# RWKV chunk recurrence: the right-hand side of the solve as one 128-row product, alphas and state copied beside masked keys and values

## What is computed

```python
def step(S, inp):
    r_t, k_t, v_t, w_t, kk_t, a_t = inp
    sa = jnp.einsum('bhij,bhj->bhi', S, -kk_t)
    S = S * w_t[:, :, None, :] + sa[..., None] * (kk_t * a_t)[:, :, None, :] + v_t[..., None] * k_t[:, :, None, :]
    return S, jnp.einsum('bhij,bhj->bhi', S, r_t)
```

## Time and profile before

| | us |
|---|---|
| median of 3 runs | 1393.52 |
| lowest and highest of them | 1392.38 and 1394.54 |
| the profiled execution | 1392.71 |
| its span, first to last instruction | 1390.9 |
| stretch of the recurrence | about 540 to 716 |

### The profile page before, as it was taken

The page is one execution under the profiler, slowest core; times in us unless marked ns, Lnnn a source line. Parts: engine busy times, 40 slices in busy tenths (PEclk is TensorE's granted clock), DMA queues, the critical chain, the costliest instruction groups (busy, mean ns, idle before and its releaser), DMA issues.

```text
span 1390.9 us, 28090 instructions
## 1 busy us (share of the span) xinstructions
PE 1329.4 (96%) x12121; PEld 987.0 (71%) x12121; DVE 700.9 (50%) x1122; ACT 491.5 (35%) x797; POOL 176.8 (13%) x216
## 2 busy tenths in 40 slices
PE   5899999999999997999999999999999999998997
PEld 1789999999999997888888998844444444433443
DVE  3423235553326665655676667725455444454454
ACT  2423235545665555555544343211000100000113
POOL 2000000000112333333433001000000000000000
PEclk9999999999999999999989999999999999999999
DMA  9557522225532220000243565999999999999993
GB/s 331 194 197 235 174 78 76 77 76 147 150 110 77 76 61 26 4 4 4 67 128 97 172 214 181 333 408 408 409 428 425 426 427 428 424 427 426 426 428 152
DMA packets 132920, 310.62 MB, mean 223 GB/s; under 512 B 13314, under 2 KB 98536, under 8 KB 119864
## 3 DMA queue, kind: packets, MB, share of 16 engines
q1 hardware_dynamic: 122078, 285.86, 54.6%
q10 hardware_dynamic: 7546, 15.58, 3.1%
q0 software_dynamic: 3168, 7.33, 1.5%
HBM read 299.88 MB, written 12.79 MB: 225 GB/s over the span
## 4 chain that ended last, share of the span: by engine, by line
PE 49%; DMA 7%; DVE 2%; ACT 1%; issue 1%; SPq 0%; DVEq 0%; ACTq 0%; POOLq 0%
PE bank L3039 13%; PE bank L2858 7%; PE bank L3063 6%; DMA lower<-in_expert_w_up 4%; PE bank L3083 4%; PE bank L2886 3%; DMA upper7b<-in_expert_w_up 2%; PE bank L1778 2%; PE bank L498 2%; PE bank L3050 1%; PE bank L3013 1%; ACT upper L1575 1%; PE bank L1844 1%; PE bank L1825 1%; PE bank L1776 1%
## 5 line engine op out<-in xcount | busy, mean ns | idle before, releaser
L953 PE MATMUL bank<-upper2end 128*128 128x272 f32 x3168 | 413.7, 291 | 5.6 <-DVE upper2end L1183 5.4
L953 PEld LDWEIGHTS bank<-upper2end 128*128 128x128 f32 x3168 | 402.1, 189 | 20.1 <-issue 19.0
L3039 PE MATMUL bank<-upper7b 128*64 128x512 f32 x784 | 230.7, 596 | 7.3 <-issue 4.2
L1160 DVE TENSOR_TENSOR upper2end<-upper,upper2end 128x1024 fp32r<-128x1024 f32 x66 | 84.8, 1284 | 250.1 <-ACT upper2end L718 249.9
L3039 PEld LDWEIGHTS bank<-upper7b 128*64 128x64 f32 x784 | 69.8, 137 | 116.5 <-issue 116.2
L3039 PE MATMUL bank<-lower,upper7b 128*64 128x512 f32 x240 | 108.6, 596 | 2.3 <-issue 1.0
L2726 ACT ACTIVATE lower<-bank 128x256 f32<-128x256 f32 x32 | 12.3, 384 | 273.6 <-PE bank L3050 273.6
L3063 PE MATMUL bank<-upper7b,lower 128*64 128x512 f32 x352 | 106.3, 595 | 0.9 <-DVE lower L3486 0.9
L3551 DVE TENSOR_TENSOR lower<-lower,bank 128x1024 f32<-128x1024 f32 (+1 forms) x70 | 82.8, 1215 | 45.4 <-PE bank L3083 42.9
L2858 PE MATMUL bank<-upper_r 128*128 128x272 f32 (+2 forms) x768 | 103.1, 293 | 0.0
L2858 PEld LDWEIGHTS bank<-upper_r 128*128 128x128 f32 x768 | 98.9, 191 | 2.9 <-issue 1.5
(11 more groups left out here) (445 smaller groups left out, 1867.4 us busy)
## 6 DMA issues: line engine op xcount, KB each, us to landing
upper7b<-in_expert_w_gate SPq DMA_DIRECT2D x20, 2048.0 KB, 23.4
upper7b<-in_expert_w_up SPq DMA_DIRECT2D x19, 2048.0 KB, 28.6
upper7b<-in_expert_w_down SPq DMA_DIRECT2D x19, 2048.0 KB, 24.3
upper<-in_w_in SPq DMA_DIRECT2D x66, 512.0 KB, 3.8
lower<-in_w_ada SPq DMA_DIRECT2D x23, 1024.0 KB, 6.9
lower<-in_expert_w_down SPq DMA_DIRECT2D x7, 2048.0 KB, 24.9
lower<-in_expert_w_gate SPq DMA_DIRECT2D x6, 2048.0 KB, 22.3
lower<-in_expert_w_up SPq DMA_DIRECT2D x6, 2048.0 KB, 28.8
```

What stands on the lines that cost most here:

```text
L953: m = mm(psum[s][:, c, 0:HALF], w_part[s][:, k, :], h_part[:, k, c * HALF:(c + 1) * HALF], start=k == 0 and w_part is w_high and h_part is ...
L1160: ve.tensor_tensor(w_rest[u % 2], w_slot[u % 2], w_high[u % 2].bitcast(F32), ALU.subtract).then_inc(w_split, 1)
L3039: m = nc.tensor.matmul(GU_BANK[s][64 * b:64 * b + 64, :], x_t[:, k, s * BLK:(s + 1) * BLK], w[:, k, :], start=k == 0, stop=k == KD - 1)
```

## The change

`by_values` and `by_state` become one group, `first_solved`: 16 products over all 128 rows. For that the alphas are copied by GpSimd into the value half's free partner block of `z4` (`alphas_stacked`), and the state is copied by VectorE into the matching block of `kbv` (`state_stacked`). The block of `z4` that is overwritten held the strictly masked products of which `off_left` reads a part, so GpSimd first copies that part into a new tile `e_off`. New semaphore `z_stacked` counts the GpSimd copies; `s_done` now counts three a chunk (the two copies and the state's last step). What waited for `mv_mm` waits for `u0_mm`.

```diff
@@ masked
-                v.wait_ge(mv_mm, c - 1)
+                v.wait_ge(u0_mm, c - 1)
@@ recurrence_gpsimd
+            def alphas_stacked(c):
+                pool.wait_ge(z_out, 4 * c + 4)
+                if c < NCH:
+                    if c:
+                        pool.wait_ge(inv_mm, inv_count(c - 1, "C1"))
+                    for h in range(2):
+                        r = QUADS[2 * h]
+                        pool.tensor_copy(e_off[r], z4[c % 2][r, :, h, 32:CH]).then_inc(z_stacked, 1)
+                    pool.wait_ge(z_stacked, 4 * c + 2)
+                for h, p in enumerate(HEADS):
+                    pool.tensor_copy(z4[c % 2][p, :, h, 0:CH], ari[c % 3][p, :, 0:CH]).then_inc(z_stacked, 1)
+                pool.wait_ge(z_stacked, 4 * c + (2 if c == NCH else 4))
+
...
             keys(1)
+            alphas_stacked(0)
             queries(1)
             for c in range(NCK):
                 if c + 1 < NCK:
                     first_sum(c + 1)
                 if c + 2 < NCK:
                     keys(c + 2)
+                if c + 1 < NCK:
+                    alphas_stacked(c + 1)
+                if c + 2 < NCK:
                     queries(c + 2)
@@ recurrence_vector
+            def state_stacked(c):
+                v.wait_ge(kbv_out, 4 * c + 4)
+                if c == NCH:
+                    v.wait_ge(entry_kept, 2)
+                elif c:
+                    v.wait_ge(s_done, 3 * c)
+                else:
+                    v.wait_ge(fixed, 4)
+                for h, p in enumerate(HEADS):
+                    nc.vector.tensor_copy(kbv[c % 2][p, :, h, CH:P], s_in(c)[p]).then_inc(s_done, 1)
...
             power(0, 4)
+            state_stacked(0)
...
                     power(c + 1, 4)
+                    state_stacked(c + 1)
                     inverse(c + 1)
@@ recurrence_tensor
             def off_left(c):
                 pe.wait_ge(t11_out, c + 1)
-                pe.wait_ge(z_out, 4 * c + 4)
+                pe.wait_ge(z_stacked, 4 * c + 2)
...
-                        m = mm(one_bank(5, CH)[o, j, 0:32], z4[c % 2][r, j, h, 32:CH], t11[r, j], start=True, stop=True)
+                        m = mm(one_bank(5, CH)[o, j, 0:32], e_off[r, j], t11[r, j], start=True, stop=True)
...
-            def by_values(c):
-
+            def first_solved(c):
                 pe.wait_ge(kbv_out, 4 * c + 4)
                 pe.wait_ge(z_out, 4 * c + 4)
+                pe.wait_ge(z_stacked, 4 * c + (2 if c == NCH else 4))
+                pe.wait_ge(s_done, 3 * c + 2)
...
                 for j in range(8):
-                    for h in range(2):
-                        r, o = HEADS[1 - h], HEADS[h]
-                        m = mm(one_bank(6, CH)[o, j], z4[c % 2][r, j, h, 0:CH], kbv[c % 2][r, j, h, CH:P],
-                               start=j == 0, stop=False, skip_group_check=True)
-                m.then_inc(mv_mm, 1)
-
-            def by_state(c):
...
-                        m = mm(one_bank(6, CH)[p, j], a[p, j, 0:CH], s_in(c)[p, j], start=False, stop=True,
-                               skip_group_check=True)
+                    for h, p in enumerate(HEADS):
+                        m = mm(one_bank(6, CH)[p, j], z4[c % 2][:, j, h, 0:CH], kbv[c % 2][:, j, h, CH:P],
+                               start=True, stop=True)
                 m.then_inc(u0_mm, 1)
...
-                by_state(c)
+                first_solved(c)
...
-                    by_values(c + 1)
```

More of the change, by code:

```diff
@@ L447, in build @@
         s_h = [S6.take(8, CH), s_second]
+        e_off = S6.take(8, 32)
         st_rows_in = z4[1][0:64].rearrange("i j h n -> i (j h n)")[:, 0:D].rearrange("i (j n) -> i j n", n=P)
@@ L1367, in build @@
         inv_mm = sem("inv_mm")
-        mv_mm = sem("mv_mm")
+        z_stacked = sem("z_stacked")
         u0_mm = sem("u0_mm")
@@ L1648, in alphas @@
                 if c >= 2:
-                    v.wait_ge(s_done, c - 1)
+                    v.wait_ge(s_done, 3 * (c - 1))
                 nc.vector.tensor_copy(lam_end[c % 2], lam_c[:, :, CH - 1]).then_inc(end_done, 1)
@@ L1807, in by_values @@
                     pe.wait_ge(entry_kept, 1)
-                    pe.wait_ge(fixed, 4)
                 for j in range(8):
-                    for h in range(2):
-                        r, o = HEADS[1 - h], HEADS[h]
-                        m = mm(one_bank(6, CH)[o, j], z4[c % 2][r, j, h, 0:CH], kbv[c % 2][r, j, h, CH:P],
-                               start=j == 0, stop=False, skip_group_check=True)
-                m.then_inc(mv_mm, 1)
-            def by_state(c):
[L1817 to L1824, removed]
-                        m = mm(one_bank(6, CH)[p, j], a[p, j, 0:CH], s_in(c)[p, j], start=False, stop=True,
-                               skip_group_check=True)
+                    for h, p in enumerate(HEADS):
+                        m = mm(one_bank(6, CH)[p, j], z4[c % 2][:, j, h, 0:CH], kbv[c % 2][:, j, h, CH:P],
+                               start=True, stop=True)
                 m.then_inc(u0_mm, 1)
@@ L1879, in recurrence_tensor @@
             power(0, 5)
-            by_values(0)
             off_left(0)
@@ L1884, in recurrence_tensor @@
                 if not more:
-                    pe.wait_ge(s_done, NCH)
+                    pe.wait_ge(s_done, 3 * NCH)
                     state_turned(0)
-                by_state(c)
+                first_solved(c)
                 if c < NCH:
@@ L1911, in recurrence_tensor @@
                         diagonal_blocks(pe, c + 2)
-                    by_values(c + 1)
                     if c + 1 < NCH:
                         off_left(c + 1)
-            pe.wait_ge(s_done, NCK)
+            pe.wait_ge(s_done, 3 * NCK)
             state_turned(1)
```

## The result

The changed kernel takes 1398.25 us in the median of 20 executions (1391.63 to 1400.65), against 1393.93 for the kernel before in 20 executions taken beside them (1388.96 to 1396.78). The ratio is 1.0028, with a 95% interval of 1.0019 to 1.0037: slower by 0.28%, or about 4. The forecast was 1390.5, faster by 3, with a range that ended at 1395.0. So the time moved the other way.

The account below looks back on a forecast made before the run. The prediction took TensorE, busy for 96% of the span, as the bound. Its terms, -3.5 chunks, +1.5 start, -0.1 last chunk and -0.9 pauses, gave -3.0, so 1390.5, with a range of 1386.3 to 1395.0.

Parts of the forecast that it names:

- The mechanism in the chunks: Chunks 1 to 7: one group less, partly lost to waits for VectorE and GpSimd; 0.5 saved each, 3.5 in all.
- the hold-up by GpSimd: Chunks 1 to 7: GpSimd's copies delay `first_solved` by 0.25, or by nothing if they go first.
- The price of a 128-row group: TensorE: `first_solved` costs what `by_state` cost, so nine groups of 1.08 go, 9.7 at most.
- The pauses of issue: TensorE's dense stretch from power 5 to `off_right`: fewer pauses, 0.9 saved in all, between nothing and 4.9.
- sign of being wrong: Middle chunks: the forecast would be wrong if the chunk period fell by over 0.9.
- The start: Chunk 0: state copies ahead of VectorE's other work delay `off_left(0)`; 1.5 lost, between 0.5 and 1.75.
- the rival on the clock: Recurrence's ends: more idle time, one more or sooner fall to 1.2 GHz for 3.5, 1.7 lost; chance 0.04 to decide the sign.
- GpSimd as the bound: Between `keys` and `first_solved`: four copies over 2.3 make it slower, 1397 or 1405; chance 0.09.
- a 128-row group at double price: TensorE: two heads' 64-row products overlap, 128-row ones don't, so nothing is saved and the time is 1395; chance 0.02.
- the full gain (case 1): Recurrence: copies don't hold each other off, 0.69 saved per chunk, half the pauses go; 6.9 faster, 1386.6; chance 0.17.

Follow-up runs that it names:

- filler at the start only: Changed kernel, chunk 0's state copies behind its inverse, constant products in waits at the recurrence's start and ahead of `off_left(0)`, none in chunks 1 to 7; ratio 0.9981 to before.
- no copies: Changed kernel without the four GpSimd and two VectorE copies and their waits, so its results are wrong; ratio 0.9997 to before, median 1393.44.
- copies moved: Changed kernel with the state copies of chunk 0 behind its inverse on VectorE instead of ahead; ratio 1.0013 to before, median 1395.09.
- the moved group: Kernel before the change with `by_values` of chunks 1 to 8 behind `off_left` instead of ahead; ratio 1.0023, median 1396.85 beside 1394.34.
- the head filler: Products of constants in TensorE's long waits at the recurrence's start; added alone to the kernel before: ratio 0.9991, median 1394.03.
- the copies with the old products: Changed kernel with all copies kept but the two 64-row groups `by_values` and `by_state` back at their old places; ratio 1.0031 to before, median 1398.11.
- filler in chunks 1 to 7: Changed kernel with overwritten products of constants, 4 ahead of `off_left` and 8 ahead of power 5, in chunks 1 to 7; ratio 1.0011 to before, median 1396.01.
- filler everywhere: Changed kernel, chunk 0's state copies behind its inverse, constant products in waits at the recurrence's start, ahead of `off_left(0)` and in chunks 1 to 7; ratio 0.9963, median 1389.33.

## Why the prediction was wrong

**The mechanism in the chunks was right.** The wait of `off_left` for the transpose was 0.32 (my 0.39), the hold-up by GpSimd 0.15 (my 0.25), so the period without pauses fell from 18.06 to 17.53, 0.53 where I had taken 0.5. A state copy takes 0.399 when nothing is in the way, for which I had 0.4. The price of a 128-row group was that of a 64-row one. GpSimd's four copies took 2.34 from the first start to the last end (600.14 to 602.48), where I had 2.0. But I had them wait for the end of the state copies, and they started ahead of it, so they were ready 0.35 sooner against power 5 than I had said (2.69 behind its start, not 3.04).

**The pauses of issue were mis-sized.** I gave 0.9 for all seven chunks. In the trace of the change nearly all are gone (one of 0.24 is left): six chunks took 6.0 less, of which 3.2 is the period and 2.8 the pauses. That is 1.0 a chunk, over the 0.9 that I had set as a sign of being wrong. Where the old products came back with the copies in place, the pauses came back too. What makes them is not shown.

**The start was right as a wait, and wrong as a price.** I said 1.5 lost by the place of the state copies, and `off_left(0)` came 1.54 later, the delay of `alphas(1)` included. That the wait itself grew from 0.24 to 2.55 says less, since `by_values(0)` no longer fills 1.08 of it. But a fall of the clock came with it, and the stretch lost 5.1. The fall's part is 4.1 to 4.7: the stretch from power 5 of chunk 0 to that of chunk 1 took 24.10 (552.94 to 577.04) with a fall and the state copies moved, and 19.44 (553.06 to 572.50) without a fall in the run with filler at the start only, with `off_left(0)` 2.1 behind power 5 in both; the change has 25.11, and 25.11 - 19.44 - 1.54 = 4.1. The two parts are together 0.5 more than the 5.1, since the kernel before had a pause of issue of 0.66 there and the change has none.

**The step that failed is the rival on the clock.** My sum had no term for the clock. As a rival I had it as a matter of the two ends of the recurrence, one fall of some 3.5 more or less, worth 1.7, and gave it 0.04. What the runs showed in its place are two falls in the change, of 13.5 and 10, that cost 4.1 and 4.4 (the chunk at 655 took 21.97 for 17.53). Without these 8.5 the recurrence would be some 6 shorter than before in these traces, not 2.4 longer. And one of the falls comes in the middle of the recurrence, where I had looked for nothing, since TensorE idles there for 0.64 and 0.32 at most.

I counted `by_values` by its time alone. It also stood between two runs of 32-column products and covered a wait, and with it gone there stand in a row the wait of 0.64, power 5, the diagonal blocks, a wait of 0.32 and `off_left`. Six traces have that row with nothing in it (twice the change, no copies, copies moved, the moved group, filler at the start only). All six have a fall that begins between power 5 of chunk 1 and that of chunk 8, and in all six the group of 64-column products behind `off_left` is the first at half clock. Seven traces have a group or filler in that row (three of the old products in their place, one of these with the head filler; the copies with the old products; filler in chunks 1 to 7 three times). None has a fall that begins there. These are single executions, and the mean clocks of the run with filler in chunks 1 to 7 alone say that some of its other executions had more falls than the traced one.

That the falls cost the change its gain is shown: in its traces the groups inside them take 1.98 where others take 1.15, and the change with its state copies of chunk 0 moved and its idle moments filled is faster than before by 0.24% to 0.51% (5 executions, with mean clocks of 0.990 to 0.993). What makes the clock fall is not shown. That it is the row of small products rather than the sum of idle time is only likely; the moved-group run points to it but is explained by its exposed wait for two thirds.

Of the other rivals: GpSimd as the bound, and a 128-row group at double price, did not occur. Of the full gain (case 1) the pauses went, even more than it had, while the period gained 0.53 and not 0.69. That gain was given back.

## What to carry to other kernels

Where the profile shows that the granted clock falls and rises within a kernel, as here, a group of products may have a second value beside its time: it may keep the clock up. Before removing one from a stretch with short waits, look at what stands in a row once it is gone, and check the granted clock by stretch after the change, not the mean. If busy time does not fall with the instruction count, look at the clock first; a few products of constants in the waits are a cheap test and can be the repair. And one trace is one execution: compare the mean clocks of all of them before trusting the place of a fall.

## What was not expected of the hardware

- A fall of the clock came without any wait over 0.64, and at a repeating place: behind `off_left` of chunk 5 in both traces of the change (655.5 and 653.5), though the traces started the recurrence 1.4 apart. In the four other traces with the same row of small products it came in chunk 1 or 6.
- Falls lasted 3.5, 7, 10 to 10.5 or 13.5, and nothing here shows what decides between them.
- The same instructions behind the same wait can run at either level. The filler at the head ran at half clock in two of its three traces and at the full clock in the third. The two rows show its first group with filler everywhere, then with filler at the start only:

```profile
542.08 1.97 PE L1899 MATMUL bank<-lower 64*64 64x64 f32 x32 [2.54 <-PEq L55]
```

```profile
540.93 1.15 PE L1899 MATMUL bank<-lower 64*64 64x64 f32 x32 [2.53 <-PEq L55]
```

- A VectorE copy within SBUF took 0.399 alone and up to 1.384 when it met a product of GpSimd. The Trainium skill, SBUF — State Buffer, Who interferes with whom, states that a VectorE copy can take a port pair that it shares with GpSimd, that whichever of the two issues first holds the pair for its whole instruction, and that the other waits. This case's trace agrees: GpSimd's product ends at 598.81 + 1.26 = 600.07, and the two copies, issued from 598.98, end at 600.89, about two copies of 0.4 later.
